# Cached-key scores of the sampled tokens: from turned keys on TensorE to products on VectorE

## The chip, the cores and the metric

The kernel runs on one NeuronCore of one Trainium2 chip. The metric is the device time of one execution in microseconds (us). Time before: median 1513.4 us of 3 runs (1511.74 to 1521.02).

## The reference

One inference step of a two-layer decoder trunk, once for a prompt of 512 tokens and once for 8 sampled tokens (one new token for each of 8 sequences, each with a cache of 512 past keys and values). Layer one is a state-space mixer with a gate; layer two is dilated attention with three groups of windows. Only the sampled tokens' attention is touched by the change:

```python
def dilated_sample_attn(q, slopes, n_strides, dilation, k_all, v_all, n_buf):
    rows = n_buf + jnp.arange(t_new)[:, None] - j[None, :] * dilation
    ...
    scores = jnp.einsum('bthd,btjhd->bhtj', q.astype(jnp.float32), kg) * (1.0 / math.sqrt(dh))
    scores = scores - slopes * (j * dilation)
    ...
    lse = jax.nn.logsumexp(scores, axis=-1)
    o = jnp.einsum('bhtj,btjhd->bthd', jnp.exp(scores - lse[..., None]), vg)
```

There are 16 heads of 64, and the three groups have (window, dilation) = (128, 1), (512, 4), (2048, 16). For each sequence the score of a head and a cached key is a dot product over 64 numbers. Group 0 needs the last 128 cached keys; groups 1 and 2 take theirs from the 128 keys that lie at every fourth position.

## The kernel before, in words

The program is a row of stages: state-space layer, gate, output projection, then `mixer` (line 1539) with the whole attention layer but its last projection, then that projection and the write-out. The change lies in `mixer` alone. Its first part projects keys and values (tiles 0 to 15). Then comes the part that matters: 32 tiles of the projection `b_w_in`, 24 query tiles (`Q0` = 16 onward; tile Q0+3f+g is query group g of head pair f) and 8 gate tiles (`Z0` = 40 onward). Weights of a tile are 512 KB. They come by DMA from the SP queue (`load`, line 98, which waits until POOL has finished with the buffer), are split in a high part by ScalarE (line 104) and a low part by GpSimd (line 109), and are used in 48 matmuls (line 1937).

All query tiles share one accumulator, `acc[0]`. PE may start the next tile only after ScalarE has copied the last one out (`q_tile`, lines 2187, 2188) and raised a semaphore (line 2192).

Between the matmuls of a tile PE does the attention of the prompt. A tile has three **slots**, after weight blocks 2, 5 and 7 (i = 0, 1, 2). A head pair f has 8 **units** u = 0 to 7, at slots 9(f+1)+u; slot 9(f+1)+8 has none, so that a head pair is a **period** of nine slots or three tiles, and runs one period behind its query tiles. For a unit

- PE forms the scores of units u and u+1 together in the slots of even u (`scores`, lines 1818, 1822), into two banks, after DVE has read the banks' last contents;
- DVE adds the distance bias and takes the minimum (`bias`, lines 2015, 2019, 2024), in the slot of the unit;
- ScalarE takes the exponential (`exps`, line 2207), DVE the reciprocal of the sum one slot later (`invert`, line 2030), GpSimd scales (lines 1767, 1769);
- PE turns the probabilities three slots later (line 1832), ScalarE moves them (line 2215), and once in a period PE multiplies with the values (lines 1842, 1847) and DVE moves the result (line 2034).

Each engine's program order is written out by the same loops over tiles and slots. On ScalarE `q_tile` stands at the start of slot i = 2, behind the exponential of the unit of slot i = 1. On DVE everything of a slot comes before everything of the next.

Beside it the sampled tokens' scores are formed for the same head pair, one sequence per unit. The SP queue loads cached keys for four sequences at a time (`decode_rows`, line 1712: key position on partitions, two tables of 128 keys). In each unit's slot PE turns the two tables (`turn_keys`, line 1907), ScalarE moves them to SBUF (`move_keys`, line 2163), and one slot later PE multiplies them with that sequence's query columns (`key_scores`, lines 1914, 1915). Once in a period ScalarE moves the scores of 8 sequences out (line 2167) to `d_scoresT`, which is read after tile Z0+3.

Once in a period ScalarE also issues a copy of 4 MB of cache from DRAM to DRAM (line 2250), at the end of each third query tile.

## Time and profile before

| | us |
|---|---|
| median of 3 runs | 1513.4 |
| profiled execution, its own time | 1511.33 |
| span of the profiled execution | 1509.5 |
| busy in it: PE / DVE / ScalarE / GpSimd | 1353.4 / 601.7 / 503.1 / 481.5 |
| mean granted TensorE clock (no time; 1 is full speed) | 0.963 |

The span is what the rows of the trace cover; the time of the execution is 1.8 us more. The query and gate tiles of `mixer` lie between 1053 and 1408. The views used are the page, the groups by line, the waits, the timeline of one engine, and the table of stretches. In a timeline each row is a run of equal instructions: its start, the time from the first's start to the last's end, how many there were, and in brackets how long the engine had been idle before them and who ended that.

### The profile page before, as it was taken

The page shows a single profiled execution, that of the slowest core. Times are in us where ns is not written, and L with a number is a line of the kernel's source. Part 1 is how long each engine was busy: PE and PEld are TensorE (multiplying, and loading weights), DVE is VectorE, ACT ScalarE, POOL GpSimd, SP SyncE. Part 2 cuts the span into 40 slices and gives each one's busy share as a digit, 9 for nine tenths or more (in the row PEclk, how much of TensorE's full clock was granted, in tenths as well). Part 3 has the DMA queues.
Part 4 walks back from the last instruction along what each step waited for, and adds up shares of the span by engine and source line. Part 5 has one row for each costly group of instructions (what it writes and reads, how often), then busy time and mean ns, then how long its engine had stood idle before and what let it go on. Part 6 is the DMA issues. An engine that isn't in the chain of part 4 may idle for free. (4 is left out here: it accounts for less than half of the span.)

```text
span 1509.5 us, 29925 instructions
## 1 busy us (share of the span) xinstructions
PE 1353.4 (90%) x12309; PEld 1286.1 (85%) x12309; DVE 601.7 (40%) x1025; ACT 503.1 (33%) x884; POOL 481.5 (32%) x296
## 2 busy tenths in 40 slices
PE   4988869979989999999997996799889999999893
PEld 4978869969889999999997995799778888889692
DVE  5855569949611211212210007552133333443314
ACT  4233233325512222222211213233355544545221
POOL 2221210000033444434433330233256555555130
PEclk9999989989989999999998998899989999999997
DMA  8588754421223333333331251143756666563211
GB/s 185 91 133 138 138 92 131 142 77 33 61 78 111 99 104 98 111 95 106 98 104 57 85 139 28 47 134 107 234 176 199 229 197 224 182 224 99 99 56 57
DMA packets 251817, 181.06 MB, mean 120 GB/s; under 512 B 44248, under 2 KB 239536, under 8 KB 250960
## 3 DMA queue, kind: packets, MB, share of 16 engines
q1 hardware_dynamic: 250928, 146.27, 37.7%
q10 hardware_dynamic: 800, 33.53, 6.1%
q8 instruction: 64, 1.05, 0.3%
q14 instruction: 25, 0.20, 0.0%
HBM read 159.49 MB, written 53.77 MB: 141 GB/s over the span
## 5 line engine op out<-in xcount | busy, mean ns | idle before, releaser
L109 POOL TENSOR_TENSOR w_lo<-raw,w_hi 128x1024 fp32r<-128x1024 f32 x154 | 368.2, 2393 | 845.7 <-ACT w_hi L104 564.6
L161 PE MATMUL acc<-act_hi,w_hi 128*128 128x256 f32 x1728 | 354.2, 286 | 21.6 <-POOL w_lo L109 10.2
L161 PE MATMUL acc<-act_lo,w_hi 128*128 128x256 f32 x1728 | 351.9, 285 | 0.0
L161 PE MATMUL acc<-act_hi,w_lo 128*128 128x256 f32 x1728 | 351.6, 285 | 0.0
L161 PEld LDWEIGHTS acc<-act_hi,w_hi 128*128 128x128 f32 x1728 | 271.7, 191 | 24.4 <-issue 16.4
L104 ACT ACTIVATE w_hi<-raw 128x1024 fp32r<-128x1024 f32 x156 | 164.8, 1057 | 382.1 <-PE acc L161 289.6
L161 PEld LDWEIGHTS acc<-act_hi,w_lo 128*128 128x128 f32 x1728 | 271.8, 191 | 0.0
L161 PEld LDWEIGHTS acc<-act_lo,w_hi 128*128 128x128 f32 x1728 | 271.7, 191 | 0.0
L1364 DVE SCALAR_TENSOR_TENSOR sig<-acc,vec,sig 128x520 f32<-128x520 f32 x16 | 12.1, 758 | 295.1 <-PE acc L161 295.1
L1937 PE MATMUL acc<-act_hi,w_hi 128*128 128x256 f32 (+1 forms) x512 | 111.7, 300 | 9.9 <-ACTq L2192 9.7
L1937 PE MATMUL acc<-act_lo,w_hi 128*128 128x256 f32 (+1 forms) x512 | 103.5, 284 | 0.0
L1937 PE MATMUL acc<-act_hi,w_lo 128*128 128x256 f32 (+1 forms) x512 | 103.4, 283 | 0.0
L2015 DVE SCALAR_TENSOR_TENSOR scores<-near_distances,neg_slopes,acc 128x256 f32<-128x256 f32 x64 | 30.3, 474 | 178.9 <-PE acc L1822 178.9
L1937 PEld LDWEIGHTS acc<-act_hi,w_hi 128*128 128x128 f32 x512 | 79.4, 191 | 17.7 <-ACTq L2192 13.9
L1769 POOL TENSOR_SCALAR scores<-scores,prob_scale 128x384 f32<-128x384 f32 x64 | 79.6, 1244 | 6.3
L1937 PEld LDWEIGHTS acc<-act_lo,w_hi 128*128 128x128 f32 x512 | 80.1, 190 | 0.0
L1937 PEld LDWEIGHTS acc<-act_hi,w_lo 128*128 128x128 f32 x512 | 79.8, 189 | 0.0
L2215 ACT ACTIVATE probsT<-aux 128x384 f32<-128x384 f32 x64 | 31.4, 491 | 108.3 <-PE aux L1832 89.0
L1767 POOL TENSOR_TENSOR scores<-scores 128x128 f32<-128x128 f32 x64 | 29.4, 460 | 110.1 <-DVE prob_scale L2030 110.1
L161 PE MATMUL acc<-y_hi,w_hi 128*128 128x256 f32 (+1 forms) x256 | 54.1, 293 | 10.0 <-issue 6.1
L2207 ACT ACTIVATE scores<-scores,neg_max 128x512 f32<-128x512 f32 x64 | 46.4, 724 | 29.8 <-DVE neg_max L2024 29.5
L161 PE MATMUL acc<-y_lo,w_hi 128*128 128x256 f32 (+1 forms) x256 | 53.0, 289 | 0.0
(314 smaller groups left out, 2019.1 us busy)
## 6 DMA issues: line engine op xcount, KB each, us to landing
raw<-a_w_glu SPq DMA_DIRECT2D x64, 512.0 KB, 4.1
s_kv<-cache_kv ACTq DMA_DIRECT2D x8, 4088.0 KB, 16.4
raw<-a_w_in SPq DMA_DIRECT2D x32, 512.0 KB, 4.3
raw<-b_w_in SPq DMA_DIRECT2D x32, 512.0 KB, 4.4
raw<-a_w_out SPq DMA_DIRECT2D x16, 512.0 KB, 3.8
raw<-w_kv SPq DMA_DIRECT2D x16, 512.0 KB, 4.1
k_rows<-cache_kv SPq DMA_DIRECT2D x32, 256.0 KB, 7.4
v_rows<-cache_kv SPq DMA_DIRECT2D x16, 512.0 KB, 7.1
```

Source lines behind the costliest of these rows:

```text
L104: act.activation(self.mem.wh[s][:, :, :], self.mem.raw[s][:, :, :], ACT.Copy).then_inc(self.hi_ready, 1)
L109: pool.tensor_tensor(self.mem.wl[s][:, :, :], self.mem.raw[s][:, :, :], self.mem.wh[s][:, :, :].bitcast(F32), ALU.subtract).then_inc(self. ...
L161: ins = nc.tensor.matmul(mem.acc[a][:, 256 + lo:256 + hi], w[s][:, k, :], x[:, k0 + k, lo:hi], start=first and k == 0 and i == 0, stop=las ...
L1364: v.scalar_tensor_tensor(sg[s][:, :], columns(mem.acc[1]), mem.vec[:, bass.ds(V_BGLU + i, 1)], sg[s][:, :], ALU.add, ALU.mult).then_inc(dn ...
L1767: pool.tensor_tensor(x[:, 2, :], x[:, 2, :], x[:, 3, :], ALU.add).then_inc(scaled, 1)
L1769: pool.tensor_scalar(x[:, 0:3, :], x[:, 0:3, :], linv[:, i:i + 1], None, ALU.mult).then_inc(scaled, 1)
L1937: ins = nc.tensor.matmul(acc[a][:, 256 + lo:256 + hi], w[t % 2][:, k, :], x[:, k, lo:hi], start=k == 0 and i == 0, stop=k == 7 and i == 2)
L2015: v.scalar_tensor_tensor(x[:, 0:2, :].rearrange("p a k -> p (a k)"), near[:, r, :], slope[:, head:head + 1], src[:, 0:256], ALU.mult, ALU. ...
L2207: act.activation(x, x, ACT.Exp, scale=-1.0, bias=nmin[:, i:i + 1], accum_out=lsum[:, i:i + 1]).then_inc(exped, 1)
L2215: act.activation(PT[h][:, r, :, :], aux[n % 2][:, 0:3 * P].rearrange("p (c x) -> p c x", c=3), ACT.Copy).then_inc(p_moved, 1)
```

## The change

The keys are no longer turned. The three query rows of a head pair for 8 sequences (24 rows of 128) are turned by PE in two matmuls (`turn_q`), moved by ScalarE, and stored to DRAM (12 KB). Two DMAs (`spread_q`) read 12 of these rows each and write them to all 128 partitions, 6 KB a partition, 768 KB a DMA. DVE then multiplies key rows with spread query rows (128x512 a group and half) and sums over the 64 numbers of a head (`score_keys`: 48 products and 48 reductions in all). They stand in the slots of units 5, 6, 7, none, 0 and 1, each behind that slot's `bias` and `invert`. The SP queue gains the store and the two spreads in each period, and the order of its key loads changes; ScalarE waits for the scores before it overwrites their buffers with gate tiles; PE waits for them once, after tile Z0+3.

```diff
@@ SP queue
             def decode_rows(m):
-                f, s, i = m // 2, 4 * (m % 2), m % 2
+                f, s, i = m // 2, HALF * (m % 2), m % 2
...
-                    sp.wait_ge(kt_full, 4 * m - 4)
+                    sp.wait_ge(scored, 3 * m - 3)
...
+            def store_q(f):
+                sp.wait_ge(qr_moved, f + 1)
+                sp.dma_start(dram["q"][f, :, :], qrow[:, :]).then_inc(qr_out, 16)
+
+            def spread_q(f):
+
+                sp.wait_ge(qr_out, 16 * f + 16)
+                for h in range(2):
+                    if f:
+                        sp.wait_ge(scored, 6 * f - 3 + 3 * h)
+                    to = qb[spread_at(2 * f + h)]
+                    sp.dma_start(to[:, :, :, :], dram["q"][f:f + 1, 3 * HALF * h:3 * HALF * h + 3 * HALF, :]
+                                 .rearrange("o (s g) d -> o s g d", g=3).broadcast_to([P, HALF, 3, P])
+                                 ).then_inc(qb_in[h], 16)
...
-            rows_at = {Q0 + 5 + 3 * f: f for f in range(1, DT)}
+            rows_at = {Q0 + 6 + 3 * f: f for f in range(DT)}
...
                 if t in rows_at:
-                    decode_rows(2 * rows_at[t])
+                    store_q(rows_at[t])
+                    if rows_at[t]:
+                        decode_rows(2 * rows_at[t])
                 if t - 1 in rows_at:
-                    decode_rows(2 * rows_at[t - 1] + 1)
+                    f = rows_at[t - 1]
+                    if f == DT - 1:
+                        sp.wait_ge(s_full, 8 * (DT - 1))
+                    spread_q(f)
+                    if f:
+                        decode_rows(2 * f + 1)
...
@@ PE
-            def turn_keys(n):
...
-            def key_scores(n):
...
+            def turn_q(f):
+                pe.wait_ge(q_ready, 3 * f + 3)
+                pe.wait_ge(smp_moved if f == 0 else qr_moved, max(f, 1))
+                for e in range(2):
+                    ins = nc.tensor.matmul(aux[3][0:3 * NS, 0:P], qs[:, f, :, :, e].rearrange("p s g -> p (s g)"),
+                                           mem.ident[:, :], start=e == 0, stop=e == 1)
+                ins.then_inc(qr_full, 1)
...
-                    n = unit_at.get(slot - 1)
-                    if n is not None:
-                        key_scores(n)
-                    if slot in unit_at:
-                        turn_keys(unit_at[slot])
-                        if unit_at[slot] % 2 == 0:
-                            scores(unit_at[slot])
+                    if slot % 9 == 0 and 0 < slot <= 9 * DT:
+                        turn_q(slot // 9 - 1)
+                    if slot in unit_at and unit_at[slot] % 2 == 0:
+                        scores(unit_at[slot])
...
@@ DVE
+            def score_keys(m, g):
+                f, h = divmod(m, 2)
+                if g == 0:
+                    v.wait_ge(d_in[h], 32 * f + 32)
+                    v.wait_ge(qb_in[h], 16 * f + 16)
+                v.tensor_tensor(prod[:, g, :, :], krow[h][:, :, min(g, 1), :], qb[spread_at(m)][:, :, g, :],
+                                ALU.mult).then_inc(multiplied, 1)
+                v.wait_ge(multiplied, 3 * m + g + 1)
+                v.tensor_reduce(scT[:, g, HALF * h:HALF * h + HALF, 2 * f:2 * f + 2],
+                                prod[:, g, :, :].rearrange("p s (e d) -> p s e d", e=2), AX_X,
+                                ALU.add).then_inc(scored, 1)
...
+    score_at = {9 * f + 14 + i: (2 * f + i // 3, i % 3) for f in range(DT) for i in range(6)}
...
+                    if slot in score_at:
+                        score_keys(*score_at[slot])
...
@@ ACT
-            def move_keys(n):
...
+            def move_q(f):
+                act.wait_ge(qr_full, f + 1)
+                if f:
+                    act.wait_ge(qr_out, 16 * f)
+                act.activation(qrow[:, :], aux[3][0:3 * NS, 0:P], ACT.Copy).then_inc(qr_moved, 1)
...
+                act.wait_ge(scored, 6 * DT - 6 if f < 3 else 6 * DT)
                 act.activation(zb[:, f, :], x, func).then_inc(done, 1)
```

DVE, units 5 and 6 of a period, before. `neg_max` is the end of `bias`, `prob_scale` is `invert`:

```order
L2015 SCALAR_TENSOR_TENSOR scores_6433<-near_distances,neg_slopes,acc 128x256
L2019 SCALAR_TENSOR_TENSOR scores_6433<-far_distances,neg_slopes,acc 128x128 x2
L2024 TENSOR_REDUCE neg_max<-scores_6433 128x1
L2030 RECIPROCAL prob_scale<-prob_sum 128x1
L2015 SCALAR_TENSOR_TENSOR scores_6434<-near_distances,neg_slopes,acc 128x256
L2019 SCALAR_TENSOR_TENSOR scores_6434<-far_distances,neg_slopes,acc 128x128 x2
L2024 TENSOR_REDUCE neg_max<-scores_6434 128x1
L2030 RECIPROCAL prob_scale<-prob_sum 128x1
```

The same place after the change:

```order
L2025 SCALAR_TENSOR_TENSOR scores_6433<-near_distances,neg_slopes,acc 128x256
L2029 SCALAR_TENSOR_TENSOR scores_6433<-far_distances,neg_slopes,acc 128x128 x2
L2034 TENSOR_REDUCE neg_max<-scores_6433 128x1
L2040 RECIPROCAL prob_scale<-prob_sum 128x1
L2062 TENSOR_TENSOR d_products<-k_rows_6459,q_spread_6457 128x512
L2065 TENSOR_REDUCE d_scoresT<-d_products 128x4x2
L2025 SCALAR_TENSOR_TENSOR scores_6434<-near_distances,neg_slopes,acc 128x256
L2029 SCALAR_TENSOR_TENSOR scores_6434<-far_distances,neg_slopes,acc 128x128 x2
L2034 TENSOR_REDUCE neg_max<-scores_6434 128x1
L2040 RECIPROCAL prob_scale<-prob_sum 128x1
L2062 TENSOR_TENSOR d_products<-k_rows_6459,q_spread_6457 128x512
L2065 TENSOR_REDUCE d_scoresT<-d_products 128x4x2
```

A product and a reduction now stand between one unit's bias and the next one's, and the first of them in a period waits for key rows and spread queries.

SP queue, one period, before:

```order
L98 DMA raw_56<-b_w_in 128x8x128
L98 DMA raw_57<-b_w_in 128x8x128
L1712 DMA k_rows_6456<-cache_kv 128x4x128
L1712 DMA k_rows_6456<-cache_kv 128x4x128
L98 DMA raw_56<-b_w_in 128x8x128
L1712 DMA k_rows_6457<-cache_kv 128x4x128
L1712 DMA k_rows_6457<-cache_kv 128x4x128
```

The same three loads of weights after the change:

```order
L98 DMA raw_56<-b_w_in 128x8x128
L1720 DMA scratch_q<-q_rows 24x128
L1715 DMA k_rows_6459<-cache_kv 128x4x128
L1715 DMA k_rows_6459<-cache_kv 128x4x128
L98 DMA raw_57<-b_w_in 128x8x128
L1729 DMA q_spread_6457<-scratch_q 128x1536
L1729 DMA q_spread_6456<-scratch_q 128x1536
L1715 DMA k_rows_6460<-cache_kv 128x4x128
L1715 DMA k_rows_6460<-cache_kv 128x4x128
L98 DMA raw_56<-b_w_in 128x8x128
```

The first half's keys go one tile later, behind the store of the queries; the second half's also go one tile later, behind both spreads.

## Rows read from the trace of the kernel before

**Rows 1.** Table of stretches, four periods: length, busy us by engine, clock, DMA share, GB/s.
```profile
1225.20:1260.00 34.80, 33.66 (x357) 30.04 (x357) 14.88 (x42) 18.16 (x46) 20.51 (x20) 1.00 0.63 195
1260.00:1297.40 37.40, 34.08 (x358) 30.20 (x358) 14.86 (x42) 18.22 (x46) 20.53 (x20) 1.00 0.67 227
```

**Rows 2.** Timeline of PE, one unit's work for the sampled tokens, in slot of unit 3.
```profile
1201.91 0.28 PE L1914 MATMUL aux<-q_sample,d_keysT 128*128 128x2 f32 x2
...
1202.53 0.49 PE L1832 MATMUL aux<-ident,scores 128*128 128x128 f32 x3
```

**Rows 3.** Timeline of PE, the landmarks of one period.
```profile
1228.75 0.55 PE L1832 MATMUL aux<-ident,scores 128*128 128x128 f32 x3
1235.63 0.51 PE L1937 MATMUL acc<-act_hi,w_hi 128*128 128x256 f32 x2
...
1245.67 0.55 PE L1832 MATMUL aux<-ident,scores 128*128 128x128 f32 x3
1249.34 0.51 PE L1937 MATMUL acc<-act_hi,w_hi 128*128 128x256 f32 x2 [0.72 <-ACTq L2192]
1253.54 0.55 PE L1832 MATMUL aux<-ident,scores 128*128 128x128 f32 x3
1259.78 0.51 PE L1937 MATMUL acc<-act_hi,w_hi 128*128 128x256 f32 x2 [0.41 <-ACTq L2192]
```

**Rows 4.** Timelines of DVE and ScalarE behind the score pair of units 6 and 7.
```profile
1253.64 0.48 DVE L2015 SCALAR_TENSOR_TENSOR scores<-near_distances,neg_slopes,acc 128x256 f32<-128x256 f32 x1 [3.25 <-PE acc L1822]
1255.35 0.46 DVE L2015 SCALAR_TENSOR_TENSOR scores<-near_distances,neg_slopes,acc 128x256 f32<-128x256 f32 x1
1256.36 0.69 DVE L2024 TENSOR_REDUCE neg_max<-scores 128x1 f32<-128x512 f32 x1
1257.87 0.72 ACT L2207 ACTIVATE scores<-scores,neg_max 128x512 f32<-128x512 f32 x1
1258.67 0.37 ACT L2187 ACTIVATE q_sample<-acc 64x8 f32<-64x8 f32 x2
```

**Rows 5.** Timeline of DVE late in the mixer, GpSimd idle: a product of two 128x512 SBUF tiles.
```profile
1400.87 0.68 DVE L2040 TENSOR_TENSOR attn_out<-attn_out,zb 128x512 f32<-128x512 f32 x1
```

**Rows 6.** Line 320 (ns min/median/max), and its like, line 330, beside GpSimd.
```profile
L320 DVE SCALAR_TENSOR_TENSOR norm_kv_tmp<-xT,vec,norm_kv_rstd x8: 754/759/762, 934.6 to 943.8; 128x520 f32<-128x520 f32 x8
976.83 2.74 DVE L330 SCALAR_TENSOR_TENSOR norm_kv_tmp<-xT,vec,norm_kv_rstd 128x520 f32<-128x520 f32 x1
976.61 2.40 POOL L109 TENSOR_TENSOR w_lo<-raw,w_hi 128x1024 fp32r<-128x1024 f32 x1 [11.92 <-ACT w_hi L104]
```

**Rows 7.** Timeline of GpSimd behind the slot of unit 5.
```profile
1252.25 2.38 POOL L109 TENSOR_TENSOR w_lo<-raw,w_hi 128x1024 fp32r<-128x1024 f32 x1
```

**Rows 8.** Timeline of the SP queue: one load of weights and one of key rows.
```profile
1241.76 0.37 SPq L98 DMA_DIRECT2D raw<-b_w_in  x1
1264.27 10.48 SPq L1712 DMA_DIRECT2D k_rows<-cache_kv  x1
```

**Rows 9.** The page, part 6: DMA issues, KB each, median us to landing.
```profile
raw<-b_w_in SPq DMA_DIRECT2D x32, 512.0 KB, 4.4
v_rows<-cache_kv SPq DMA_DIRECT2D x16, 512.0 KB, 7.1
```

**Rows 10.** Table of stretches around tile Z0+1 (columns as in Rows 1).
```profile
1350.00:1354.00 4.00, 2.24 (x30) 1.59 (x29) 0.00 (x0) 0.47 (x2) 0.55 (x1) 1.00 0.90 256
1354.00:1356.00 2.00, 2.00 (x21) 1.76 (x14) 0.86 (x3) 0.02 (x1) 0.00 (x0) 0.55 0.06 11
1356.00:1358.00 2.00, 2.00 (x12) 2.00 (x12) 1.97 (x6) 1.56 (x4) 0.89 (x2) 0.60 0.00 0
```

**Rows 11.** Waits from 1050 to 1415: who for whom, us in total, times, longest.
```profile
PE aux L1907 <- DMA k_rows<-cache_kv: 8.3, 8, 1.9
PE aux L1914 <- ACT d_keysT L2163: 6.4, 1, 6.4
```

**Rows 12.** Timeline of ScalarE in the first period.
```profile
1097.16 1.06 ACT L104 ACTIVATE w_hi<-raw 128x1024 fp32r<-128x1024 f32 x1 [7.48 <-DMA raw<-b_w_in]
```

More of the change, by code:

```diff
@@ L1580, in mixer @@
     st, o = mem.at("d_stats", [P, 4], o)
-    keysT = []
-    for s in range(2):
-        t, o = mem.at(f"d_keysT{s}", [P, 2 * P], o)
-        keysT.append(t)
-    krow = []
-    a = mem.actl_at + 4 * TOK * 4
-    for s in range(2):
-        t, a = mem.at(f"k_rows{s}", [P, 4, 2, P], a)
-        krow.append(t)
+    prod, o = mem.at("d_products", [P, 3, HALF, P], o)
+    qrow, _ = mem.at("q_rows", [3 * NS, P], 1408)
+    qb = [mem.at(f"q_spread{n}", [P, HALF, 3, P], at)[0]
+          for n, at in enumerate((mem.actl_at, mem.actl_at + 3 * TOK * 4, q_at))]
+    at, a = mem.at("k_rows0", [P, HALF, 2, P], mem.actl_at + 3 * TOK * 4 + 3 * HALF * P * 4)
     assert a <= mem.actl_at + DT * TOK * 4
+    krow = [at, mem.at("k_rows1", [P, HALF, 2, P], vt_at)[0]]
     V = []
@@ L1634, in slot_of, with spread_at @@
         return SLOTS * (t - Q0) + i
+    def spread_at(m):
+        return 2 if m == 2 * DT - 1 else (m + 1) % 2
+    score_at = {9 * f + 14 + i: (2 * f + i // 3, i % 3) for f in range(DT) for i in range(6)}
     unit_at = {}
@@ L1666, in mixer @@
         smp_full, smp_moved, new_kv = sem("sample_rows"), sem("sample_rows_moved"), sem("new_kv_stored")
-        d_in, kt_full, kt_moved = [sem("d_rows_in0"), sem("d_rows_in1")], sem("d_keys_turned"), sem("d_keys_moved")
-        sT_full, sT_moved, zeroed, qk = sem("d_scoresT"), sem("d_scoresT_moved"), sem("q_sample_zeroed"), sem("qk_new")
+        d_in, qb_in = [sem("d_rows_in0"), sem("d_rows_in1")], [sem("q_spread0"), sem("q_spread1")]
+        qr_full, qr_moved, qr_out = sem("q_rows_full"), sem("q_rows_moved"), sem("q_rows_stored")
+        multiplied, scored, zeroed, qk = sem("d_multiplied"), sem("d_scored"), sem("q_sample_zeroed"), sem("qk_new")
         c_in, v_in, vn_in = sem("d_constants_in"), [sem(f"v_in{s}") for s in range(NS)], sem("v_new_in")
@@ L1757, in _ @@
                 sp.dma_start(mem.raw[n][:, :, :], nxt.first[n]).then_inc(nxt.landed[n], 16)
+            sp.wait_ge(scored, 6 * DT)
             for n in range(12, 2 * NS):
@@ L1896, in turn_new_kv @@
                                     mem.ident[:, :]).then_inc(smp_full, 1)
-            def turn_keys(n):
-                f, s = divmod(n, NS)
-                m = n // 4
-                if n == 0:
-                    pe.wait_ge(smp_moved, 1)
-                if s == 0 and f:
-                    pe.wait_ge(sT_moved, f)
-                pe.wait_ge(d_in[m % 2], 32 * (m // 2) + 32)
-                for z in range(2):
-                    ins = nc.tensor.transpose(aux[3][:, cols(z)], krow[m % 2][:, s % 4, z, :], mem.ident[:, :])
-                ins.then_inc(kt_full, 1)
-            def key_scores(n):
-                f, s = divmod(n, NS)
-                pe.wait_ge(kt_moved, n + 1)
-                at = 2 * P + 6 * s
-                nc.tensor.matmul(aux[3][:, at:at + 2], keysT[n % 2][:, 0:P], qs[:, f, s, 0, :], start=True, stop=True)
-                ins = nc.tensor.matmul(aux[3][:, at + 2:at + 6], keysT[n % 2][:, P:2 * P],
-                                       qs[:, f, s, 1:3, :].rearrange("p g e -> p (g e)"), start=True, stop=True)
-                ins.then_inc(sT_full, 1)
+            def turn_q(f):
[5 more added lines that the diff above has]
+                ins.then_inc(qr_full, 1)
             dn.start(pe)
@@ L1960, in _ @@
                 if t == Z0 + 3:
-                    pe.wait_ge(sT_moved, DT)
+                    pe.wait_ge(scored, 6 * DT)
                     pe.wait_ge(p_moved, UNITS - 1)
@@ L2238, in _ @@
                         move_probs(n)
-                    n = unit_at.get(slot - 1)
-                    if n is not None and n % NS == NS - 1:
-                        move_scoresT(n // NS)
+                    if slot % 9 == 1 and 1 < slot <= 9 * DT + 1:
+                        move_q(slot // 9 - 1)
                     n = unit_at.get(slot)
                     if n is not None:
-                        move_keys(n)
                         exps(n)
```

10 lines of the change are left out of this document (1 added, 9 removed).

## The prediction

> **What bounds the kernel now.** I read the table of stretches first, cut at one period (nine slots, three tiles) of a head pair. PE is busy 33.66 of 34.80 us while DVE has 14.88 and GpSimd 20.51 [rows 1], so PE's work sets a period, and its timeline says what that work is. One unit of the sampled tokens costs PE 0.62 us: from 1201.91, where the score matmuls start, to 1202.53, where the next work starts behind the two key transposes [rows 2]. With 64 units that is 39.7 us; with the waits of PE for key rows (8.3 us) and for one moved key tile (6.4 us) [rows 11] it is 54 us, the most that the change could give. To see how much of it lies on the path I name landmarks in the timeline of PE [rows 3]. T0, T4 and T6 are the ends of the score pairs of units 0, 4 and 6 (1228.75, 1245.67, 1253.54); B2, B5 and B8 are the starts of the tiles behind the slots 2, 5 and 8 of the period (1235.63, 1249.34, 1259.78). So T0 to B2 is 6.88 us, B2 to T4 10.04, T4 to B5 3.67, B5 to T6 4.20, T6 to B8 6.24, and the rest of the 34.80, B8 to the next T0, is 3.77.
>
> A tile can start only when ScalarE has moved the last one out, and that stands behind the exponential of the slot before, which waits for DVE. The timelines of DVE and ScalarE [rows 4] give this chain: 0.10 from the score pair to the first bias (1253.54 to 1253.64), 1.71 for it with its reciprocal, 1.70 for the second bias, 0.80 for the exponential, 1.11 for moving the query tile (1258.67 to 1259.78). Behind T4 only one bias is in it: 0.10 + 1.71 + 0.80 + 1.11 = 3.72, and T4 to B5 is 3.67, with an idle PE (0.72) [rows 3]. **That boundary is set by the chain already**, and the PE work that goes from it gives nothing. Behind T0 and T6 two biases are in it: 5.42 us, below the 6.88 and 6.24 that PE needs now.
>
> **The change part by part.**
> - *PE work out, between chains.* B2 to T4 holds two whole slots of it (2 x 0.62 = 1.24), B5 to T6 one (0.62). Both are on the path: -1.86 a period.
> - *PE work in.* Two matmuls of 24 rows at slot 0, in place of that slot's two key transposes. No row shows them; the transposes are their nearest kin, and both are two matmuls of 128 columns with the same identity. I take 0, between -0.25 and +0.6.
> - *DVE work in.* A product of 128x512 in SBUF is 0.68 [rows 5], a reduction of 128x512 is 0.69 [rows 4]: 1.37 a pair, 6 a period, 48 in all, 66 us. DVE has room (14.88 + 8.2 of 34). What counts is the place. One pair stands between the biases of units 0 and 1, one between those of 6 and 7. These two chains become 5.42 + 1.37 = 6.79. T0 to B2: 6.79 in place of 6.88, -0.09, although 1.24 of PE work leaves it. T6 to B8: 6.79 in place of 6.24, **+0.55**. Without waits a period is -1.86 - 0.09 + 0.55 = -1.40.
> - *ScalarE work out.* 64 moves of keys. They lie beside PE's matmuls; the chain above is already written without them.
> - *Waits of PE on key rows.* 8.3 us, of which 1.9 at the first, so 0.9 a period on the mean [rows 11]; the period with 37.40 [rows 1] has 2.2 of them. DVE waits for the same rows now, but with slack except at unit 5's product. I take -0.9; bounds -0.9 and 0.
> - *The spread in time?* The load of weights ahead of it goes out at 1241.76 [rows 8], 6.1 us behind B2, since it waits for GpSimd's split; the change does not move this. The spreads follow at +6.5. A 512 KB load of the same queue lands in 4.4 us alone and in 7.1 in a row of its like [rows 9]. The spread has 768 KB and stands behind 512 KB, so I take 7.1: it lands at B2+13.6. DVE has done the bias of unit 5 about 0.9 us behind B5, that is at B2 + 8.80 + 3.67 + 0.9 = B2+13.4. So the first product comes just in time; it may start 0.9 later still without touching T6 (B5 + 3.58, less 1.37 for the pair).
> - *DVE against GpSimd.* The same DVE operation on SBUF operands takes 0.76 with GpSimd idle and 2.74 when it starts 0.2 us after GpSimd's 2.40 us split [rows 6]: it waits until that ends. A new product has two SBUF operands too. GpSimd's split of weights starts 2.9 us behind B5 (1252.25) and lasts 2.38 [rows 7], so a product that comes in time goes before it, and one 1.5 us late goes behind it. The biases read PSUM and kept their 0.48 [rows 4]. For the two products inside chains I take 0.65 us a period together, from 0 up to 2.4.
> - *The clock.* T6 to B8 has 5.83 us of PE work now (6.24 less 0.41 idle [rows 3]); 1.0 of it leaves (one unit and one pair of score matmuls), the chain is 6.79 or more, so PE is idle for 2 us or more in one piece, once a period. The only such place in the steady part is tile Z0+1: PE was idle 1.76 of 4.00 us, and then the granted clock was 0.55 and 0.60 for 4 us, about half speed [rows 10]: 2 x 0.45 + 2 x 0.40 = 1.7 us lost. The idle 0.72 brought nothing. I take every second period, +0.85; bounds 0 and +1.7.
> - *Sum of a period:* -1.40 - 0.90 + 0.65 + 0.85 = -0.8; seven of them, -5.6.
> - *The first period.* ScalarE waits 7.48 us for weights until 1097.16 [rows 12], which is what PE's 6.4 us wait is. PE would get further before it stops, but the first spreads stand behind 16 small stores and two loads of weights on the SP queue, and DVE waits for them. I take 0, from -5 (stall overlapped) to +4 (spread later than that).
> - *Gate tiles.* The wait at Z0+1 goes and with it the 1.7 us at half speed: -1.7. The last products (slot 82) are behind T6 by 0.65 + 2 x 1.7 + 5 x 1.37 + 0.94 = about 12 us, and PE comes to its new wait after Z0+3 at about 13: hidden, with 1 us to spare.
> - *SP queue.* The store of queries waits for ScalarE in slot 1, some 4 us behind the load ahead of it; the key loads behind it go out later, and the next weights have 12 us until then. Hidden. 4 MB of copy run at that time: if they hold the key loads (10.48 us for one issue [rows 8]), the spread is late; that is the third rival.
>
> Total: -5.6 + 0 - 1.7 = -7.3. The profiled execution took 1511.3, so the changed one would take **1504**. The median of the runs is 1513.4, 2 us above it: the range is put round 1504 with this in its upper part.
>
> **The rivals.**
> 1. *The gain lands.* No half speed, products never behind GpSimd, the first period's stall overlapped: 7 x (-1.40 - 0.90) - 1.7 - 5 = -22.8, 1489. For it: the margins above are near zero, not negative, and idle pieces of 0.41 and 0.72 us did no harm. Against: one idle piece of 2 us a period is new. By the Trainium skill (DMA: Bandwidth & Descriptors, the section on the anatomy of one DMA) a DMA costs about 2.0 us and its bytes at 436 GB/s, fitted on another queue than this one; the estimate for 768 KB is 3.8 us, which would put the spread well in time. The landing times in this trace are longer.
> 2. *GpSimd holds the products.* If both products of the chains wait for GpSimd by 1.2 us (it is busy 20.5 of 34.8 us [rows 1]), a period has +2.4 in place of +0.65, and the longer idle brings the half speed each time: -1.40 - 0.90 + 2.4 + 1.7 = +1.8, seven of them +12.6, less 1.7: 1522. By the Trainium skill (SBUF — State Buffer, who interferes with whom) a VectorE instruction with two SBUF inputs and a GpSimd instruction that reads SBUF exclude each other for their whole length; the trace agrees, 0.76 against 2.74.
> 3. *The spread comes late (slower).* Place: the product of unit 5, which DVE has in front of the bias of unit 6. From 0.9 us behind the forecast on, every us moves T6 to B8 by one, and from 1.5 us on GpSimd's split adds up to 2.4. If the copy and the key loads hold the spread by 3 us, the chain has +2.1 + 1.2, and with half speed each time a period is -1.40 - 0 + 3.3 + 1.7 = +3.6: +25, with +4 in the first period less 1.7, 1539. It decides for slower from about 2.5 us lateness. For it: a key load's issue stood for 10.48 us. Against: by then the copy has landed in most periods.
> 4. *The spread does not run like a load.* All its packets read the same 6 KB of DRAM, and no row shows such a read. At half the rate of the weights it is case 3 and worse, 1550 or more.
>
> **How the numbers follow.** Forecast 0.44 (own range 1496 to 1514), the gain lands 0.24, GpSimd holds 0.14, late 0.13, slow spread 0.05. A measurement of this kernel can tell about 1% (15 us) from no change. Faster by over 1% (below 1498): nearly all of the first rival and a little of the forecast, 0.26. Slower by over 1% (above 1526): the late and the slow spread and a part of GpSimd's, 0.19. Within: 0.55. From 1486 to 1532 leaves out the deep end of the first rival and the longer half of the third and fourth.
>
> **What would show it.** Right: PE's idle before B8 is 2 us or more and ends on ScalarE's semaphore behind the exponential; T4 to B5 is 3.7 as before; the product of unit 5 starts within 1 us of that unit's reciprocal; products are 0.7 or, next to a split, up to 3 us; some stretches at clock 0.5 between 1120 and 1370; periods of 33.5 to 35.5. Wrong: periods under 33 with a clock of 1.00 throughout (rival 1), or DVE idle for us before the first product of a period on a DMA, and periods over 36 (rivals 3, 4). If the last products come after the end of slot 83, PE's wait there is longer than I say.

## The result, and the profile after

The changed kernel takes 1496.6 us (median of 4 runs, 1494.06 to 1499.59), against 1512.57 us (4 runs) for the kernel before on the same chip: a ratio of 0.989, interval [0.986, 0.992], so 16 us or 1.1% less, between 0.85% and 1.4%. The forecast was 1504, its range 1486 to 1532. The profiled execution after took 1499.59 us, 3 us above its median; its span is 1497.8 us, 11.7 less than before. In it the stretch from the second query tile to the first matmul of the next stage is 345.5 us long (1064.16 to 1409.67), where it was 355.3. So 9.8 us lie in this stretch. Another 3.5 us lie ahead of it, where nothing was changed, and 1.6 us are lost again behind it; both are taken as chance. The pair of traces thus shows less than the medians do.

From the page after: the busy times of part 1, two groups of part 5 (busy us, mean ns, idle time before and who ended it), and two rows of part 6 (KB each, median us to landing):

```profile
PE 1324.4 (88%) x11957; PEld 1256.3 (84%) x11957; DVE 669.6 (45%) x1121; ACT 484.5 (32%) x820; POOL 493.5 (33%) x296
...
L1950 PE MATMUL acc<-act_hi,w_hi 128*128 128x256 f32 (+1 forms) x512 | 113.3, 304 | 33.0 <-ACTq L2210 29.3
...
L1793 POOL TENSOR_TENSOR scores<-scores 128x128 f32<-128x128 f32 x64 | 39.4, 616 | 92.2 <-DVE prob_scale L2040 92.2
...
q_spread<-scratch_q SPq DMA_DIRECT2D x16, 768.0 KB, 7.4
...
k_rows<-cache_kv SPq DMA_DIRECT2D x32, 256.0 KB, 8.3
```

PE has 29 us less to do, DVE 68 us more. PE stands idle 29.3 us for the query tile's buffer (line 2210), where it stood 9.7 us before (line 2192). GpSimd's masking step on line 1793 grew from 0.46 to 0.62 us on the mean. The table of stretches, cut at B8 as in [rows 1] (length, PE, PE's loads, DVE, ScalarE, GpSimd busy, granted clock, DMA share, GB/s):

```profile
1113.09:1149.12 36.03, 31.88 (x312) 27.64 (x313) 22.63 (x55) 15.96 (x37) 22.04 (x20) 0.92 0.71 235
1149.12:1184.30 35.18, 31.02 (x312) 27.19 (x312) 22.65 (x55) 15.96 (x37) 22.03 (x20) 0.95 0.78 256
1184.30:1218.04 33.74, 29.59 (x312) 25.67 (x312) 22.83 (x55) 15.96 (x37) 22.13 (x20) 1.00 0.82 280
1218.04:1251.56 33.52, 29.42 (x313) 25.65 (x313) 22.86 (x55) 15.98 (x37) 21.65 (x20) 1.00 0.83 272
1251.56:1286.90 35.34, 31.18 (x312) 27.18 (x312) 22.90 (x55) 15.96 (x37) 22.20 (x20) 0.95 0.78 264
1286.90:1320.67 33.77, 29.61 (x313) 25.64 (x313) 22.92 (x55) 15.95 (x37) 22.18 (x20) 1.00 0.82 266
```

Before, such periods were 34.80 at best and 37.40 where a key-row wait fell in [rows 1]. Now the clean ones are 33.5 to 33.8, and the other three have a granted clock of 0.92 to 0.95 and are 1.4 to 2.5 us longer. In the shortest PE is busy for 29.42 of 33.52 us; the 4.1 us of idle time stand in three pieces. The landmarks of this period in PE's timeline, answering to [rows 3]: T0, B2, T4, B5, T6, B8.

```profile
1222.18 0.55 PE L1858 MATMUL aux<-ident,scores 128*128 128x128 f32 x3
...
1228.79 0.51 PE L1950 MATMUL acc<-act_hi,w_hi 128*128 128x256 f32 x2 [0.89 <-ACTq L2210]
...
1237.62 0.55 PE L1858 MATMUL aux<-ident,scores 128*128 128x128 f32 x3
...
1241.30 0.51 PE L1950 MATMUL acc<-act_hi,w_hi 128*128 128x256 f32 x2 [1.35 <-ACTq L2210]
...
1244.88 0.55 PE L1858 MATMUL aux<-ident,scores 128*128 128x128 f32 x3
...
1251.56 0.72 PE L1950 MATMUL acc<-act_hi,w_hi 128*128 128x256 f32 x2 [1.86 <-ACTq L2210]
```

B2 to T4 is 8.83 (was 10.04), T4 to B5 3.68 (3.67), B5 to T6 3.58 (4.20), T0 to B2 6.61 (6.88), T6 to B8 6.68 (6.24), B8 to T0 4.14. For the last the prediction had 3.77, as the rest of a period cut by eye at 34.80. The tile's own row before gives 1228.75 - 1224.94 = 3.81, and so a clean period of 34.84:

```profile
1224.94 0.51 PE L1937 MATMUL acc<-act_hi,w_hi 128*128 128x256 f32 x2 [0.41 <-ACTq L2192]
```

Where the clock is full, T6 to B8 is the one distance that varies by more than 0.05: 6.68 to 6.97 in the six periods. The last row of the period above is 0.72 long where its like takes 0.51: behind the idle piece of 1.86 us PE runs at about half speed, as the table of stretches around it says:

```profile
1247.60:1251.60 4.00, 2.14 (x19) 1.90 (x17) 3.93 (x10) 2.19 (x6) 2.96 (x4) 1.00 0.89 308
1251.60:1254.60 3.00, 3.00 (x14) 3.00 (x15) 0.99 (x2) 1.44 (x2) 2.90 (x4) 0.51 1.58 637
```

DVE's timeline at the unit 5 product, the place of [rows 4]: reciprocal, product, reduction, next bias, and the product inside the chain.

```profile
1242.19 0.15 DVE L2040 RECIPROCAL prob_scale<-prob_sum 128x1 f32<-128x1 f32 x1
1243.20 0.92 DVE L2062 TENSOR_TENSOR d_products<-k_rows,q_spread 128x512 f32<-128x512 f32 x1 [0.85 <-DMA q_spread<-scratch_q]
1244.15 0.69 DVE L2065 TENSOR_REDUCE d_scoresT<-d_products 128x8 f32<-128x512 f32 x1
1244.98 0.48 DVE L2025 SCALAR_TENSOR_TENSOR scores<-near_distances,neg_slopes,acc 128x256 f32<-128x256 f32 x1
...
1246.69 0.67 DVE L2062 TENSOR_TENSOR d_products<-k_rows,q_spread 128x512 f32<-128x512 f32 x1
```

The first product of the period starts 0.86 us behind the end of the reciprocal (1242.34), all of it a wait for the spread query rows, and ends at 1244.12, just before GpSimd's split starts. GpSimd's timeline there, as [rows 7]:

```profile
1244.20 2.39 POOL L109 TENSOR_TENSOR w_lo<-raw,w_hi 128x1024 fp32r<-128x1024 f32 x1
1246.85 0.83 POOL L1793 TENSOR_TENSOR scores<-scores 128x128 f32<-128x128 f32 x1 [0.27 <-DVE prob_scale L2040]
```

When DVE's product is first (1246.69), GpSimd's step of 0.46 us takes 0.83. The SP queue around the spread, as [rows 8]:

```profile
1225.91 0.32 SPq L1720 DMA_DIRECT2D scratch_q<-q_rows  x1
1226.28 6.57 SPq L1715 DMA_DIRECT2D k_rows<-cache_kv  x2
1234.26 0.37 SPq L98 DMA_DIRECT2D raw<-b_w_in  x1
1235.48 1.31 SPq L1729 DMA_DIRECT2D q_spread<-scratch_q  x2
```

The spreads go out 6.7 us behind B2. Waits after, from 1070 to 1430 (who for whom, total, times, longest), first DVE's, then SP's from 1117 to 1410:

```profile
DVE d_products L2062 <- DMA q_spread<-scratch_q: 10.8, 5, 8.3
...
SPq L1729 <- DMA scratch_q<-q_rows: 3.5, 3, 1.5
SPq L1727 <- DMA scratch_q<-q_rows: 1.5, 1, 1.5
```

8.3 of the 10.8 us are the first product of all; the other four are 2.5 us together. In answer to [rows 11], PE has no wait for keys left. The first period's stall [rows 12] is still there and is longer: ScalarE waits 9.7 us for weights where it waited 7.5, PE 9.3 where it waited 6.4.

### The profile page after: what moved, and what is told of

Same layout as the page of the kernel before. It is cut to its first block and busy times, and to the rows that moved or that the text cites. A ratio compares the mean times of both kernels' runs of the same rounds, so it can differ in the third digit from the quotient of the medians.

```text
span 1497.8 us, 29253 instructions
## 1 busy us (share of the span) xinstructions
PE 1324.4 (88%) x11957; PEld 1256.3 (84%) x11957; DVE 669.6 (45%) x1121; ACT 484.5 (32%) x820; POOL 493.5 (33%) x296
## 5 line engine op out<-in xcount | busy, mean ns | idle before, releaser
L1950 PE MATMUL acc<-act_hi,w_hi 128*128 128x256 f32 (+1 forms) x512 | 113.3, 304 | 33.0 <-ACTq L2210 29.3
L1793 POOL TENSOR_TENSOR scores<-scores 128x128 f32<-128x128 f32 x64 | 39.4, 616 | 92.2 <-DVE prob_scale L2040 92.2
```

What stands on the lines that cost most here:

```text
L1793: pool.tensor_tensor(x[:, 2, :], x[:, 2, :], x[:, 3, :], ALU.add).then_inc(scaled, 1)
L1950: ins = nc.tensor.matmul(acc[a][:, 256 + lo:256 + hi], w[t % 2][:, k, :], x[:, k, lo:hi], start=k == 0 and i == 0, stop=k == 7 and i == 2)
```

## Experiments

All medians stand beside runs of the kernel before on the same chip, and ratios are to that; medians from different chips are not compared. "Mixer" is the stretch from the second query tile to the next stage's first matmul, "period" a distance from B8 to B8, both of the profiled execution. A "pair" is one product of DVE with its reduction.

**Both kernels again**, with no edit, for the size of scatter.

> The changed kernel once more, unaltered. The first comparison gave 1.1% (0.9856 to 0.9915), but the two traces differ by 9.8 us (0.65%) between the start of tile Q0+1 and the first matmul of the next stage, and by 11.7 us over the span, of which 3.5 lie ahead of the change. Theory A (the trace has the whole effect, the rest is chance outside the mixer): ratio 0.991 to 0.995. Theory B (the profiled pair shows too little): ratio 0.986 to 0.990, and this trace has a mixer shorter than the first one's 345.5 us by 3 us or more.

> The kernel before once more, unaltered, for a second trace of it and for what the measurement can tell. Ratio 0.997 to 1.003. From tile Q0+1 to the next stage's first matmul the first trace has 355.3 us; if that stretch is steady this one has 354 to 357 (theory A); if the periods of the kernel before differ from execution to execution by their waits for key rows, 350 to 362 (theory B).

The changed kernel: 1503.8 us, ratio 0.989 [0.985, 0.992], periods 36.0, 35.2, 33.8, 33.9, 33.6, 35.2, mixer 346.1. The kernel before: 1518.56, ratio 0.999 [0.997, 1.001], periods 34.9, 35.5, 38.5, 35.6, 39.1, 35.3, mixer 358.1 where the profile ahead of the prediction had 355.3. The changed kernel repeats within 1 us; the kernel before does not. Of a_again's two theories neither held whole: the ratio is the one of theory B, but the changed kernel's mixer is no shorter. What moved is the kernel before (theory B of b_again), and with it the difference of the mixers, from 9.8 to 12.0 us. The two long periods are those in which PE waited most for key rows: 2.5 us in one piece, and 2.9 in two pieces of 1.55 and 1.32. The table of stretches of the repeated kernel before, its third period and what follows the wait in it; then the last wait of the fifth period and what follows it:

```profile
1187.07:1225.58 38.51, 35.38 (x356) 31.31 (x356) 14.86 (x42) 18.25 (x45) 20.54 (x20) 0.96 0.66 219
...
1209.60:1213.00 3.40, 3.40 (x33) 2.70 (x18) 1.63 (x5) 0.77 (x2) 0.00 (x0) 0.51 0.01 2
```
```profile
1283.56 0.44 PE L1907 MATMUL aux<-ident,k_rows 128*128 128x128 f32 x2 [1.32 <-DMA k_rows<-cache_kv]
```
```profile
1284.70:1288.00 3.30, 3.30 (x19) 3.08 (x20) 2.23 (x6) 1.28 (x3) 0.00 (x0) 0.50 0.01 2
```

PE waited 2.51 us for key rows until 1208.86, and then had a granted clock of 0.51 for 3.4 us, which is another 1.7 us lost. Part of the 4.2 us went into slack: the period is 38.51 where 34.85 is the clean one. A wait of only 1.32 us was followed by 3.3 us at 0.50 as well.

**Products moved** (e_moved). They leave the slots of units 6 and 0, which lie in the two-bias chains, for slots behind boundaries that PE sets.

```diff
-    score_at = {9 * f + 14 + i: (2 * f + i // 3, i % 3) for f in range(DT) for i in range(6)}
+    place = {DT - 2: (0, 1, 2, 3, 4, 5), DT - 1: (0, 2, 3, 3, 4, 5)}
+    score_at = {}
+    for f in range(DT):
+        for i, at in enumerate(place.get(f, (0, 2, 3, 5, 6, 7))):
+            score_at.setdefault(9 * f + 14 + at, []).append((2 * f + i // 3, i % 3))
```

> The changed kernel with the products in other slots: those of units 6 and 0, which stand between two biases whose second one holds back the next tile, go to slots in which no tile waits for DVE (units 5, 7, none, then 1, 2, 3; the last two head pairs differ, since ScalarE waits for their scores). The same work on every engine. Chain theory: T0 to B2 falls from 6.6 to 5.4 to 5.7 (PE's own work again), T6 to B8 from 6.7 to 5.4 to 5.6, so a period from 33.6 to about 31.2, PE's idle before B8 under 1 us and no half speed there (1.7 us in two of six periods): 6 x 2.4 + 3 = 17 us less than the changed kernel, 1478 to 1483. Rival (DVE's or GpSimd's total work, or the spreads' transfers, hold the periods): 1494 to 1500, no change, with the idle before B8 still there.

1496.73, ratio 0.984 [0.980, 0.988]. The expected 17 us did not come: against a_again, on the same chip, it is 7 us. Two periods are 31.5 and 31.6, as the chains say; the rest are 32.9 to 35.4. DVE waits for the spread 18.0 us in 7 waits, and twice in the six periods a late product falls beside GpSimd's split; PE then waits 2.1 and 2.5 us for GpSimd and loses clock behind it. The two short periods bear the chain out; at the faster pace the spread is what comes late.

**Keys' work out, waits kept** (b_nokeys, in the kernel before).

```diff
-                for z in range(2):
-                    ins = nc.tensor.transpose(aux[3][:, cols(z)], krow[m % 2][:, s % 4, z, :], mem.ident[:, :])
-                ins.then_inc(kt_full, 1)
+                pe.sem_inc(kt_full, 1)
...
-                        key_scores(n)
...
-                        move_keys(n)
```

> The kernel before without the sampled tokens' key work on PE and ScalarE: the key transposes, their moves, the score matmuls and the moves of scores are left out (the cached scores are zero); the loads of key rows and PE's wait for them stay. It prices the work that the change takes from PE. By its busy sum of 0.62 us a unit: 1512 - 40 = 1472. Chain theory: part of it was hidden already (T4 to B5 stays 3.67, T6 to B8 cannot fall below 5.42): a period 31.5 with its waits for rows, 1478 to 1484, so at most 28 to 34 us were to be had and the products in place cost the rest.

1517.97, ratio 0.997 [0.995, 0.999]: about 0.3% for all of PE's key work. The expectation failed. Waits of PE, and the stretches around one of them:

```profile
PE acc L1818 <- DMA k_rows<-cache_kv: 33.2, 13, 5.3
```
```profile
1270.00:1274.50 4.50, 2.19 (x18) 1.99 (x17) 0.00 (x0) 1.14 (x3) 2.32 (x3) 1.00 0.80 222
1276.30:1279.30 3.00, 2.36 (x25) 1.36 (x26) 0.07 (x1) 0.00 (x0) 0.00 (x0) 0.50 0.15 46
```

PE came to its wait earlier and waited 33.2 us instead of 8.3 [rows 11]. Behind the one of 4.75 us shown here it had a granted clock of 0.50, and 0.50 to 0.60 behind five more of 3.3 us and longer; behind one of 2.83 us (until 1164.51) it had 1.00. With these waits kept, taking out PE's work gives next to nothing, so the work alone could not be the gain; the wait had to leave PE too. Whether another order of the key loads in the kernel before, with the work still on PE, would have removed the waits was not tried.

**No loads, with and without the work** (b_noload, b_none). Only the first two sets of key rows are loaded; b_none drops PE's and ScalarE's key work besides, as in b_nokeys.

```diff
-                if m < 2:
-                    sp.wait_ge(dn.unit_read, 2 * DT + 2)
-                else:
-                    sp.wait_ge(kt_full, 4 * m - 4)
+                if m > 1:
+                    return
+                sp.wait_ge(dn.unit_read, 2 * DT + 2)
...
-                pe.wait_ge(d_in[m % 2], 32 * (m // 2) + 32)
+                pe.wait_ge(d_in[m % 2], 32)
```

> The kernel before; of the sixteen loads of key rows only the first two are made, and every later turn and score works on those two tiles again (so the cached scores of features 1 to 7 are of the wrong rows). TensorE's key work, ScalarE's moves and all else are unchanged; gone are 14 loads of 512 KB and the waits for them. Theory A, key-row waits are what TensorE paid beside its own work (0.25 to 2.8 us each in the repeated run of the kernel before, a lowered clock behind the long ones): periods of 34.0 to 34.8 us with none above 36, 1507 to 1512 against 1518. Theory B, those waits were slack that returns as another wait: within 3 us of the kernel before.

> As b_noload, and with TensorE's turns and scores of key rows left out as well (the cached scores are zero throughout): the difference between the two is the price of TensorE's key work when no wait for key rows can take its place. Theory A, the 1.86 us of a period lie on the path as the chain of waits said: 1.9 us a period shorter than b_noload, periods of 32 to 33 us, 12 to 15 us below b_noload, so near 1495. Theory B, it is cover for a chain on VectorE and ScalarE: under 4 us between the two.

b_noload: 1509.25, ratio 0.992 [0.989, 0.995]. b_none: 1477.94, ratio 0.971 [0.968, 0.974]. A period of each, first b_noload's, then b_none's:

```profile
1188.98:1223.83 34.85, 33.70 (x357) 30.08 (x357) 14.85 (x42) 18.21 (x45) 20.56 (x20) 1.00 0.57 189
```
```profile
1206.97:1237.91 30.94, 28.79 (x309) 25.30 (x309) 14.87 (x42) 15.93 (x36) 20.54 (x20) 1.00 0.61 195
```

All six periods of b_noload are 34.8 us, the clean period of [rows 1]: the loads' traffic costs a clean period nothing, while the waits for them and the clock behind those cost 12.7 us in all by the medians, as b_noload's expectation had it (theory A). PE's key work, with ScalarE's moves beside it, costs 3.9 us a period, twice the 1.86 of the prediction: 31 us between the two kernels, where 12 to 15 was expected. PE's timeline of b_none at the landmarks T0, B2, T4, B5, T6, B8:

```profile
1210.55 0.55 PE L1831 MATMUL aux<-ident,scores 128*128 128x128 f32 x3
...
1216.20 0.51 PE L1932 MATMUL acc<-act_hi,w_hi 128*128 128x256 f32 x2
...
1225.04 0.55 PE L1831 MATMUL aux<-ident,scores 128*128 128x128 f32 x3
...
1228.70 0.51 PE L1932 MATMUL acc<-act_hi,w_hi 128*128 128x256 f32 x2 [1.34 <-ACTq L2185]
...
1232.28 0.55 PE L1831 MATMUL aux<-ident,scores 128*128 128x128 f32 x3
...
1237.91 0.51 PE L1932 MATMUL acc<-act_hi,w_hi 128*128 128x256 f32 x2 [0.81 <-ACTq L2185]
```

B2 to T4 is 8.84 and B5 to T6 3.58, each shorter by what the prediction said. But T0 to B2 is 5.65 and T6 to B8 5.63, where b_noload has the 6.88 and 6.24 of [rows 3]: 1.23 and 0.61 less. There too PE's key work was on the path, as long as no pair of DVE took its place.

**DVE's pairs out** (e_empty, in the changed kernel).

```diff
-                v.tensor_tensor(prod[:, g, :, :], krow[h][:, :, min(g, 1), :], qb[spread_at(m)][:, :, g, :],
-                                ALU.mult).then_inc(multiplied, 1)
-                v.wait_ge(multiplied, 3 * m + g + 1)
-                v.tensor_reduce(scT[:, g, HALF * h:HALF * h + HALF, 2 * f:2 * f + 2],
-                                prod[:, g, :, :].rearrange("p s (e d) -> p s e d", e=2), AX_X,
-                                ALU.add).then_inc(scored, 1)
+                v.memset(scT[:, g, HALF * h:HALF * h + HALF, 2 * f:2 * f + 2], 0.0).then_inc(scored, 1)
```

> The changed kernel with each product and each reduction of VectorE left out and a small fill of the scores put in their place (the cached scores are zero); its waits for the spread query rows and for the key rows stay. Theory A, the two pairs of 1.37 us that stand inside the two chains of softmax are paid in full: T0 to B2 falls from 6.6 to about 5.3, T6 to B8 from 6.7 to about 5.4, a clean period from 33.5 to 31 us, and 15 to 18 us off the changed kernel, near 1487, less what late spreads take back. Theory B, they are hidden: within 4 us of the changed kernel. GpSimd's split, 0.82 us beside a product, should stand at 0.46 throughout.

1486.81, ratio 0.977 [0.973, 0.980]: some 18 us below the changed kernel by the two ratios, a little more than theory A's 15 to 18 allows. A period, and GpSimd's masking step from the groups by line:

```profile
1215.31:1246.80 31.49, 29.33 (x313) 25.62 (x313) 15.01 (x48) 16.10 (x37) 20.56 (x20) 1.00 0.86 276
```
```profile
L1793 POOL TENSOR_TENSOR scores<-scores 128x128 f32<-128x128 f32 x64 | 29.5, 461 | 78.8 <-DVE prob_scale L2040 78.8
```

T0 to B2 is 5.65 (1219.44 to 1225.09) and T6 to B8 5.63 (1241.17 to 1246.80) here, so the pairs cost 0.96 and 1.05 in the changed kernel, 2.0 us a period, in place of 2 x 1.37: the other 0.4 and 0.3 us of them lie beside PE's own work. No period of e_empty has a lowered clock. Its 0.55 us above b_none is B8 to T0, 4.13 against 3.58, where the query turn stands.

**A later spread** (e_late, in the changed kernel).

```diff
-                    spread_q(f)
                     if f:
                         decode_rows(2 * f + 1)
+                    spread_q(f)
```

> The changed kernel with its second 512 KB of key rows issued ahead of the spread of the query rows instead of behind it, in every period but the first; nothing else. It is the case of a late spread made on purpose. Theory A, the spread lands with under a microsecond to spare and VectorE's queue stands behind it: each such period has a wait of 1.5 to 4 us of the first product for the spread, GpSimd's split runs into it, and the time is 8 to 20 us above the changed kernel, 1505 to 1518. Theory B, the landing is set by the spread itself or the wait has cover: within 4 us of the changed kernel.

1519.93, ratio 0.9995 [0.996, 1.003]: the whole gain is gone. DVE's, GpSimd's and PE's timelines in one period:

```profile
1219.73 2.46 DVE L2062 TENSOR_TENSOR d_products<-k_rows,q_spread 128x512 f32<-128x512 f32 x1 [2.33 <-DMA q_spread<-scratch_q]
```
```profile
1219.26 2.38 POOL L109 TENSOR_TENSOR w_lo<-raw,w_hi 128x1024 fp32r<-128x1024 f32 x1
```
```profile
1226.91 0.90 PE L1858 MATMUL aux<-ident,scores 128*128 128x128 f32 x3 [2.49 <-POOL scores L1795]
1229.39 0.81 PE L1950 MATMUL acc<-act_hi,w_hi 128*128 128x256 f32 x2 [1.58 <-ACTq L2210]
```

The product is 2.3 us late, meets the split, and takes 2.46 us instead of 0.68; it ends within 0.6 us of the split. PE is idle 2.49 and 1.58 us, then at a low clock (its tile's first row 0.81 instead of 0.51). The six periods are 35.3 to 38.4 us. This is the third rival made on purpose, and it costs 16 us against the changed kernel by the two ratios (0.0108 of 1515), or 16.6 by the mixer (362.1 against 345.5); theory A had 8 to 20.

**An earlier spread, two ways** (e_early, e_mid, both e_moved with the store of the new tokens three tiles later and the spread split in its halves). The first puts the first half ahead of the key rows, the second behind them; the second half stays where it was:

```diff
@@ e_early
                     store_q(rows_at[t])
+                    spread_q(rows_at[t], 0)
                     if rows_at[t]:
                         decode_rows(2 * rows_at[t])
@@ e_mid
                     store_q(rows_at[t])
                     if rows_at[t]:
                         decode_rows(2 * rows_at[t])
+                    spread_q(rows_at[t], 0)
```

> e_moved with two more edits: the store of the new tokens' keys and values goes behind the first key tiles' spread (three tiles later), and the first half of each spread is issued right behind the store of the query rows and ahead of the 512 KB of key rows, a tile earlier than before. Theory A, what kept e_moved from its short periods throughout was a spread that came late (waits of 2 to 3.6 us, then a low clock) and in the first period the wait behind the stores: all seven periods at 31.5 to 32.5 us, first period under 33, 8 to 14 us below e_moved, near 1485. Theory B, the late periods were held by VectorE's and GpSimd's own load at the end of the stage: no better than e_moved, 1494 to 1500.

> As e_early, but the first half of each spread is issued behind the 512 KB of key rows and ahead of the next tile's weights: no key row is delayed by it, and it still leaves about 4 us earlier than in e_moved. Theory A, in e_early the spread took the key rows' turn on the queue (products waited 2.4 us and more for key rows in every second period) and in e_moved the spread came last, so this order serves both: periods of 31.5 us in most, 1482 to 1492. Theory B, the queue has no order without a late transfer at this pace: then the weights or the key rows are late in turn, GpSimd's split lands beside a product, and the time is 1494 or more, no better than e_moved.

e_early: 1505.9, ratio 0.990 [0.987, 0.994], worse than e_moved, where 8 to 14 us better was expected. Waits of SP and DVE in it:

```profile
SPq L1732 <- DMA scratch_q<-q_rows: 59.1, 7, 10.5
```
```profile
DVE d_products L2066 <- DMA k_rows<-cache_kv: 12.3, 4, 4.1
```

From the store of the queries (12 KB) until the spread directly behind it goes out 6.4 to 10.9 us pass in the seven later periods, 9 on the mean. SP stands there, 59.1 us in all, and the key rows behind it come late. It was not their place among the bytes, as I had supposed, but the wait in front of them.

e_mid: **1487.98**, ratio 0.978 [0.975, 0.980]: 2.2% below the kernel before, and below the changed one. This is inside theory A's 1482 to 1492. Its waits of SP and DVE, and one period:

```profile
SPq L1732 <- DMA scratch_q<-q_rows: 26.8, 7, 5.8
```
```profile
DVE d_products L2066 <- DMA q_spread<-scratch_q: 4.3, 4, 1.6
```
```profile
1180.17:1211.67 31.50, 29.34 (x313) 25.63 (x313) 24.54 (x55) 16.08 (x37) 22.27 (x20) 1.00 0.93 313
```

Its first five periods are 31.5 and the sixth 32.8, all with a clock of 1.00. In e_moved both halves left 18 to 19.5 us behind B8, behind a load of weights; here the first half leaves 17.8 to 18.7 behind it but ahead of the weights. The first product waited 0.6 to 3.6 us in five of e_moved's six periods; here it waits 0.2, 0.9 and 1.6 us in three of six. The period of e_empty, 31.49, is reached with the products in. Not all of the gain over e_moved is the spread's place: some 3 us lie in the first period (44.8 us for 47.9), where the later store of the new tokens bears on the queue too.

## Why the prediction came out as it did

The sum went in the right direction and was too small: -7.3 us against -16 by the medians, with the forecast 7.4 us too high and the range holding. In the traces the mixer fell by 9.8 us in the first pair and by 12.0 in the second. The 4 to 6 us that the medians show beyond that lie in no trace, and where they are stays open. The parts of the mixer, in us (the seventh period is the first with gate tiles):

| part | forecast | first pair | second pair |
|---|---|---|---|
| first period | 0 | -0.7 | +2.1 |
| six periods | -4.8 | -7.2 | -11.2 |
| seventh period, with Z0+1 | -2.5 | -3.9 | -3.7 |
| from there to the next stage | 0 | +2.0 | +0.9 |
| sum | -7.3 | -9.8 | -12.0 |

**Two terms were mis-sized:** the waits for key rows, priced from one execution, and GpSimd's hold on the products, which was not there. By its steps:

- *A period without waits: -1.40; measured -1.32* (34.84 to 33.52), or -1.16 for the mean of the three clean periods. B2 to T4 -1.21 for -1.24, B5 to T6 -0.62 for -0.62, T4 to B5 unchanged, T0 to B2 -0.27 for -0.09, T6 to B8 +0.44 for +0.55 (+0.61 on the mean of six), B8 to T0 +0.33 for 0. The experiments say what the small numbers are made of: -3.9 for PE's key work, +0.55 for the query turn, +2.0 for two pairs: -1.35. Taken alone, the work on the path (1.86 for 3.9) and the pairs (2.74 for 2.0) were wrong by much; taken as the longer of PE's work and the chain at each landmark, they were right. That the forecast named only 1.86 of PE's work did no harm there, since the rest of it was priced in the chains.
- *The query turn: 0, bounds -0.25 and +0.6; measured +0.33* against the two transposes that it replaces. By the experiments the keys' work there was 0.23 of path (3.81 in b_noload, 3.58 in b_none) and the query turn is 0.55.
- *Waits for key rows: -0.9 a period, so -6.3, and -1.7 for the half speed behind the wait at Z0+1; together -8.0. By the medians b_noload puts them at 12.7 us (interval of its ratio, 8 to 16 us): 4.7 us more.* In the execution that [rows 11] were read from, the seven periods lie 8.7 us above b_noload's, so for it the term was right. In the repeated one they lie 12.8 above: the waits were longer, and behind them stand stretches at half clock, which the forecast had at one place only. The failing step was to take one execution's waits for the kernel's. b_nokeys shows the other side: with less work PE waits for the rows instead, so this gain came from moving the *wait*, not only the work.
- *GpSimd against DVE: +0.65; measured about 0*, 4.6 us over seven periods, and in the first pair of traces the larger miss. The products inside the two chains took 0.68 and 0.67 (1223.91, 1246.69). The chain behind T0 came out at 6.61, that behind T6 at 6.68 to 6.97, for the 6.79 that has no hold in it. The hold exists, but in the chains GpSimd was the one that stood (0.83 for 0.46), off the path. The Trainium skill (SBUF — State Buffer, who interferes with whom) has the two exclude each other for their whole length; the trace agrees in the main both ways round, 0.83 here and 2.46 beside a split of 2.38 in e_late, though the second to start ends 0.3 to 0.6 us behind the first, a little sooner than its full 0.46 or 0.68.
- *The clock: +0.85; measured +0.9.* Three of six periods were 2.4, 1.5 and 1.7 us above the mean of the clean ones, 33.68: 5.5 / 6. The idle piece ahead of B8 is 1.86 to 1.94 us, and the forecast's 2 us or more was slightly high. That the size fits is partly luck: "every second period" was a choice, not worked out. Seven such pieces end a period; behind three the clock was half (1.94, 1.93, 1.86), behind four it was 1.00 (1.93, 1.92, 1.93, 1.93). Why in these periods and not in those stays open.
- *First period: 0; measured -0.7* (start of the second tile to the first B8, 49.6 to 48.9). In the repeated pair it is +2.1 (47.0 to 49.1), so its sign stays open. The first product waited 8.3 us for its spread as feared, beside the stall for weights that was there already.
- *Gate tiles: -1.7, and -0.8 as the seventh period.* From the last B8 to the next stage -1.9 was measured in the first pair and -2.8 in the second. It is the sum of a larger gain in the seventh period and a loss behind it, whose cause is not shown; the kernel before differs by 1.3 us there from one execution to the other. PE's new wait after Z0+3 does not show.
- *The spread in time.* It left 6.7 us behind B2 for 6.5, and its product started at B2+14.4 for a landing at 13.6. The 0.9 us of slack was real: 0.85 of it was used, and B5 to T6 did not move. The landing takes 7.4 us on the median, for 7.1. By the Trainium skill (DMA: Bandwidth & Descriptors, the anatomy of one DMA), whose fit is for another queue, the 768 KB would take 3.8 us, an estimate; the rows show about twice that.
- *What I left out* is the landing of the 12 KB store, on which the spread's issue waits. By rows it is at most some 9.6 us in the period shown (1225.91 to 1235.48). Here other work covers all of it but 5.0 us in four waits, 1.5 at most. By the anatomy of one DMA in the Trainium skill (DMA: Bandwidth & Descriptors) 12 KB is about 2.0 us, an estimate; the rows show several times that.

The rivals: the gain's full landing at 1489 needed a clock of 1.00 throughout and did not come; e_mid saved more than that, 34 us by its medians, by moving the products out of the chains and the spread forward. The second did not happen. The third did not either (its place was reached, 0.85 us late of 0.9), but e_late shows that 512 KB ahead of the spread is enough for it, and e_moved that a shorter period is enough. The fourth is refuted by the landing times.

## What to carry to other kernels

Read waits from more than one execution before pricing them: two traces of the same kernel differed by 4 us here. Price a removed piece of work together with the wait that stands in front of it: if the wait is for a transfer at its own pace, taking out the work mostly lengthens the wait, and what pays is to move the wait to an engine that has time. At each boundary write down the longer of the engine's own work and the chain beside it, for before and for after; single terms taken from one of the two don't add. A small store that a later transfer depends on can be the longest item of a queue: put independent loads between the two, and not the dependent transfer directly behind it.

## What the runs showed of the hardware that was not expected

- Both DVE and GpSimd can be the one that stands: a 0.46 us step of GpSimd takes 0.83 beside a product, and a 0.68 us product 2.2 to 2.8 beside a split of 2.4. In these cases the one that started second paid.
- Sixteen DMAs, each of which reads one piece of 6 KB in DRAM 128 times, once for each partition, landed in 7.4 us on the median for 768 KB, beside 8.3 for 256 KB of key rows: here the repeated read was no slower than the strided ones.
- A store of 12 KB took 6.4 to 10.9 us until a queue that waited for it went on (1126.80 to 1135.98 in e_early; 1225.91 to 1235.48 after), with a 4 MB copy under way beside it each time. In the first period after, where no such copy had been issued for 20 us, it took 3.8 (1094.31 to 1098.12). That the copy is the cause is likely and not shown.
- The length of an idle piece alone did not say whether the clock falls. Behind pieces of 1.32 us (b_again, until 1283.56) and 1.86 us (after, until 1251.56) PE ran at a granted clock of 0.50 and 0.51; behind pieces of 1.92 us (after, until 1218.04) and 2.83 us (b_nokeys, until 1164.51) it ran at 1.00. Behind waits of 2.51 and 4.75 us it ran at half speed too. In the six periods of e_empty and the first five of e_mid, whose pieces are 1.35 us at most, it stayed at 1.00.
